# A gated mixer whose recurrence levels run between the half chunks of its input projection

## The reference, cut to what matters

```
h = rms_norm(x, mix_norm[l]) @ w_mix_in[l]                  # 256 x 1024 @ 1024 x 3336
(c_x, c_b, c_c, h_q, h_f, h_i, h_g, f_q, f_k, f_v, f_f) = split(h)
y = concat(short_conv(c_x, c_b, c_c),                       # 256 columns
           hgrn2(h_q, h_f, h_i, h_g),                       # 4 heads of 64, a gated recurrence
           fox(f_q, f_k, f_v, f_f))                         # 8 heads of 64, forgetting attention
x = x + y @ w_mix_out[l]

hgrn2:  S_t = diag(f_t) S_{t-1} + (1 - f_t)^T v_t,   o_t = q_t S_t
        out = rms_norm(o, gain) * silu(g)
fox:    q, k = rms_norm per head;   s[t, s'] = q_t . k_s' + c_t - c_s'   (c = cumsum log f)
        out = softmax(causal(s)) @ v
short_conv: c_b * causal_conv3(c_c * c_x)
```

## Time and profile before

| | us |
|---|---|
| median of 3 runs | 2005.02 |
| the profiled execution, its own time | 2008.44 |
| its span | 2007.1 |
| PE busy | 1850.7 (92%) |
| DVE busy | 1022.5 (51%) |
| ACT busy | 837.9 (42%) |
| POOL busy | 27.4 (1%) |

### The profile page before, as it was taken

One profiled execution on the slowest core, in us unless ns is written; L12 is line 12 of the kernel. 1 busy time (PEld: TensorE's weight loads), 2 busy tenths in 40 slices (PEclk: granted clock), 3 DMA queues, 4 the chain that ended last, 5 costly groups with the idle time before them and its releaser, 6 DMA issues.

```text
span 2007.1 us, 21477 instructions
## 1 busy us (share of the span) xinstructions
PE 1850.7 (92%) x8492; PEld 1453.1 (72%) x8492; DVE 1022.5 (51%) x1212; ACT 837.9 (42%) x1004; POOL 27.4 (1%) x51
## 2 busy tenths in 40 slices
PE   5998789988888999899999888999999998889999
PEld 3765667766556778688788667888888877668887
DVE  2726544324566544555455745554555457536543
ACT  3326434323344444354445434444444346325441
POOL 0000000000000000000000100000000000000000
PEclk8999799989898999999999759999999999569999
DMA  9652267745452765465554203655565554005651
GB/s 338 224 194 78 64 207 255 266 176 207 166 180 84 229 216 191 130 214 181 189 176 160 84 1 100 199 185 188 170 189 187 189 161 160 16 21 168 189 189 63
DMA packets 239597, 330.31 MB, mean 165 GB/s; under 512 B 11205, under 2 KB 192089, under 8 KB 239497
## 3 DMA queue, kind: packets, MB, share of 16 engines
q1 hardware_dynamic: 235872, 321.95, 48.6%
q10 hardware_dynamic: 2890, 5.39, 0.8%
q0 software_dynamic: 736, 1.60, 0.3%
HBM read 327.85 MB, written 1.05 MB: 164 GB/s over the span
## 4 chain that ended last, share of the span: by engine, by line
PE 82%; DVE 9%; ACT 4%; DMA 3%; issue 2%; SPq 0%; DVEq 0%; ACTq 0%
PE bank L398 16%; PE bank L400 16%; PE bank L399 16%; PE bank L675 7%; PE bank L676 7%; PE bank L678 7%; DVE lo L1666 2%; PE bank L422 2%; ACT hi L1106 2%; DMA raw<-in_ffn_w 1%; PE bank L739 1%; PE bank L927 1%; PE bank L1013 1%; PE bank L991 1%; PE bank L990 1%
## 5 line engine op out<-in xcount | busy, mean ns | idle before, releaser
L1666 DVE TENSOR_TENSOR lo<-raw,hi 128x2048 fp32r<-128x2048 f32 x258 | 590.2, 2291 | 612.2 <-ACT hi L1106 612.2
L1106 ACT ACTIVATE hi<-raw 128x2048 fp32r<-128x2048 f32 x258 | 492.3, 1912 | 477.1 <-PE bank L400 174.9
L398 PE MATMUL bank<-hi,XTh 128*128 128x512 f32 (+1 forms) x1424 | 566.7, 398 | 8.7 <-DVE XTl L1693 8.7
L399 PE MATMUL bank<-lo,XTh 128*128 128x512 f32 (+1 forms) x1424 | 554.8, 390 | 0.0
L400 PE MATMUL bank<-hi,XTl 128*128 128x512 f32 (+1 forms) x1424 | 554.8, 390 | 0.0
L398 PEld LDWEIGHTS bank<-hi,XTh 128*128 128x128 f32 x1424 | 270.4, 190 | 79.3 <-issue 14.8
L400 PEld LDWEIGHTS bank<-hi,XTl 128*128 128x128 f32 x1424 | 269.7, 189 | 56.8
L399 PEld LDWEIGHTS bank<-lo,XTh 128*128 128x128 f32 x1424 | 270.6, 190 | 52.3 <-issue 0.2
L675 PE MATMUL bank<-hi,HTh 128*128 128x512 f32 x528 | 211.0, 400 | 10.6 <-DVE HTl L1693 10.6
L676 PE MATMUL bank<-lo,HTh 128*128 128x512 f32 x528 | 208.6, 395 | 0.0
L678 PE MATMUL bank<-hi,HTl 128*128 128x512 f32 x528 | 164.8, 394 | 0.0
(11 more groups left out here) (331 smaller groups left out, 1520.4 us busy)
## 6 DMA issues: line engine op xcount, KB each, us to landing
raw<-in_ffn_w_in SPq DMA_DIRECT2D x176, 512.0 KB, 4.8
raw<-in_ffn_w SPq DMA_DIRECT2D x132, 512.0 KB, 6.0
raw<-in_ada_w SPq DMA_DIRECT2D x96, 512.0 KB, 6.1
raw<-in_ffn_w_out SPq DMA_DIRECT2D x88, 512.0 KB, 4.1
raw<-in_w_mix_in SPq DMA_DIRECT2D x52, 512.0 KB, 4.7
raw<-in_od_pw_w SPq DMA_DIRECT2D x24, 512.0 KB, 6.4
raw<-in_ev_w_in SPq DMA_DIRECT2D x20, 512.0 KB, 6.4
raw<-in_w_mix_out SPq DMA_DIRECT2D x16, 512.0 KB, 4.0
```

The costliest lines, as they stand in the source:

```text
L398: pe.matmul(dst, xh, wh, start=start, stop=False)
L399: pe.matmul(dst, xh, wl, start=False, stop=False)
L1106: act.activation(hi[r][:, :], raw[g % RING][:, :], ACT.Copy).then_inc(*up("hi", d))
L1666: dve.tensor_tensor(lo[r][:, :], raw[g % RING][:, :], hi[r][:, :].bitcast(F32), ALU.subtract).then_inc(*up("lo", d))
```

## The change

The columns of the projection are taken in another order (`MIX_COLS`): h_q and h_f first, then f_q and f_k, then c_x with c_b, c_c with h_i, and f_v; h_g is the last 256. The generators are gone: `mix` is written out on each engine, and on PE a fixed place after each half chunk holds what followed the projection before. POOL makes three of the `lo` operands (slabs d+9, d+11, d+13), and waits no longer for slab d+12 to be used. The scratch tiles `EX`, `TM`, `QKa`, `QKb` and `EXP` move out of the activation's operand `XTh` to places that are free during the projection, and `TMP` is replaced by `TN` in place.

```diff
+MIX_COLS = [(768, 1024), (1792, 2048), (2304, 2560), (0, 256), (512, 1280), (2816, 3072)]
+MIX_LAST = 1536
+
+POOL_LOW = (9, 11, 13)
...
-        EX, TM, QKa, QKb, EXP, TMP = (tile_at(f"hg_{n}", [P, 2, S], scr_at + 2048 * n) for n in range(6))
+        EX, TM = (tile_at(f"hg_e{n}", [P, 2, S], row_at + 2048 * n) for n in range(2))
+        QKa, QKb, EXP = (tile_at(f"hg_qk{n}", [P, 2, S], ht_at + 34816 + 2048 * n) for n in range(3))
...
-                jobs = background([fox_decay(l), hgrn_decay(l)])
...
+                for s in range(2, 12):
+                    c = s // 2
+                    if s % 2 == 0 and c >= 2:
+                        pe.wait_ge(*at("um_act", (l, c - 2)))
+                        pe.wait_ge(*at("um_dve", (l, c - 2)))
+                    if s == 10:
+                        pe.wait_ge(*at("c3_turned", (l, 1)))
+                    half_chunk(d + s, s % 2, x_groups(c))
+
+                    if s == 2:
+                        hgrn_turn(l)
+                    elif s == 4:
+                        fox_decay(l)
+                        pe.wait_ge(*at("hg_z", l))
+                        pe.wait_ge(*at("hg_k2t", l))
+                        hgrn_products(l, 0, K2, Q2, 4)
+                    elif s == 6:
+                        pe.wait_ge(*at("fox_c", l))
+                        hgrn_level(l, 1)
+                    elif s >= 7:
+                        hgrn_level(l, s - 5)
+                    if s == 8:
+                        pe.wait_ge(*at("um_act", (l, 3)))
+                        pe.wait_ge(*at("um_dve", (l, 3)))
+                        conv_turn(l, 1, 2)
+                    elif s == 10:
+                        pe.wait_ge(*at("um_act", (l, 4)))
+                        pe.wait_ge(*at("um_dve", (l, 4)))
+                        pe.wait_ge(*at("fox_normed", (l, 1)))
+                        fox_turn(l, 0, 0)
+                        fox_turn(l, 2, 1)
+                pe.wait_ge(*at("fox_q", (l, 0)))
+                pe.wait_ge(*at("fox_k", (l, 0)))
                 r = ready(d + 12)
...
-                for step in [h, f, h, c, f, h, c, f, h, c] + [h, f] * 16 + [f] * 20:
-                    next(step, None)
+                pe.wait_ge(*at("hg_sel", (l, 5, 1)))
+                fox_scores(l, 0)
+                fox_scores(l, 1)
...
+                hgrn_products(l, 7, K1, Q1, 2)
+                pe.wait_ge(*at("hg_sel", (l, 6, 1)))
+                fox_turn(l, 1, 4)
+                fox_turn(l, 3, 5)
...
+                conv_turn(l, 0, 0)
...
+                for u in range(N):
+                    if u + 2 < N:
+                        fox_scores(l, u + 2)
+                    if u >= 1:
+                        fox_values(l, u - 1)
+                    fox_turn_p(l, u)
+                    if u == 0:
...
+                        hgrn_products(l, 8, K1, Q1, 0, cross=True)
+                    elif u == 2:
+                        hgrn_values(l)
```

ACT's program has, at unit 6 of the loop, the gate and the root of hgrn's norm together:

```diff
+                    elif u == 6:
+                        act.wait_ge(*at("um_dve", (l, 6)))
+                        act.activation(GS[:, :, :], UM[:, :, o_hg:o_hg + HALF], ACT.Silu).then_inc(*up("hg_silu", l))
+                        act.wait_ge(*at("hg_var", l))
+                        act.activation(ST[:, 8:16], ST[:, 8:16], ACT.Sqrt).then_inc(*up("hg_std", l))
```

DVE's program, from the scan to the last chunk, and POOL's:

```diff
+                select(l, 0, 7, 4)
+                split(d + 8)
+                rows_of(2)
+                hgrn_level(l, 1)
+                hgrn_level(l, 2)
+                split(d + 10)
+                select(l, 1, 1, 6)
+                hgrn_level(l, 3)
...
+                rows_of(3)
+                select(l, 2, 2, 4)
+                hgrn_level(l, 4)
+                split(d + 12)
...
-                pool.wait_ge(*at("used", first[f"up{4 + 3 * l}"] + 12))
+                d = first[f"up{4 + 3 * l}"]
...
-                    if lv == 1:
+                    if lv == 2:
...
+                        split(d + 9)
+                    elif lv == 3:
+                        split(d + 11)
+                    elif lv == 5:
+                        split(d + 13)
```

More of the change, by code:

```diff
@@ L207, in weight_slabs @@
                 w = A["w_mix_in_2"][l, :, :]
-                chunks(f"up{p}", 6, w, 0, w, HALF, CH)
-                wide_slab(w, 3072)
+                first[f"up{p}"] = len(dense)
+                for a, b in MIX_COLS:
+                    for half in range(2):
+                        up_slab(w, a, w, b, half)
+                wide_slab(w, MIX_LAST)
                 p += 1
@@ new lines, in hgrn_products @@
+            def hgrn_products(l, i, lhs, rhs, b, cross=False):
+                for h in range(HG_H):
+                    for t in range(1 if cross else T):
+                        part = slice((h % 2) * HD, (h % 2 + 1) * HD)
+                        s_at, t_at = (0, P) if cross else (t * P, t * P)
+                        o = (2 * t + h // 2) * P
+                        last = pe.matmul(bank[b + h % 2][:, o:o + P], lhs[part, h // 2, s_at:s_at + P],
+                                         rhs[part, h // 2, t_at:t_at + P], start=True, stop=True)
+                last.then_inc(*up("hg_prod", (l, i)))
@@ L1066, in mix @@
[L1066 to L1067 removed]
+                first_chunk(p)
+                pe.wait_ge(*at("small2", (l, 2)))
+                for t in range(T):
+                    for k in range(KD):
+                        last = pe.matmul(bank[7][:, t * FOX_H:(t + 1) * FOX_H], FULL[:, k, tok[t]], WF[:, k, :],
+                                         start=(k == 0), stop=(k == KD - 1))
+                last.then_inc(*up("fox_z", l))
@@ new lines, in mix @@
+                N = len(fox_units)
+                for u in range(N):
+                    if u + 1 < N:
+                        fox_softmax(l, u + 1)
+                    if u == 0:
+                        split(d + 16)
+                    if u >= 1:
+                        fox_values(l, u - 1)
+                    if u == 2:
+                        conv_taps(l)
+                    elif u == 5:
+                        hgrn_heads(l, 0)
+                    elif u == 7:
+                        hgrn_heads(l, 1)
+                    elif u == 8:
+                        hgrn_heads(l, 2)
```

795 lines of the change are left out of this document (335 added, 460 removed).

## The result

The changed kernel takes 1973.5 us (median of four runs, 1970.5 to 1977.8), the kernel before 2006.2 in the same comparison: ratio 0.9833, 95% interval 0.982 to 0.9846, or 32.7 us less. Forecast were 23.0 us less, with a range of 1968 to 1997. The direction and the main mechanism were right and the time lies inside that range, but the gain was 1.4 times the sum, and the prediction's own narrower range, 1975 to 1990, was missed by 1.5 us.

A forecast was written before the change was run, and what follows sets the result against it. PE bounds the kernel, at the lower clock in the tails, plus about 15 us of waits there. Per mixer -23.2 + 9.1 + 2.6 = -11.5 us, -23.0 in all: 2005.0 to 1982 us; range 1975 to 1990, 8 in 10 1968 to 1997.

The forecast's parts named there:

- The clock in the projection: From the gate's products to slab d+12's end: clock 0.95 or more, levels 0 to 6 at 1.26 us each.
- the rival that it falls: Projection: small products between half chunks bring the clock down, making the kernel slower, 2014 us; chance 0.06.
- New waits, 2.6 us: Projection: PE waits for DVE's row copies before c_b's transposes, 0.9 us, and before fox's transposes, 1.7 us, each mixer.
- the first of the two places: Projection, c_b's transposes after half chunk 8: PE waits 0.9 us for chunk 3's row copy behind the norm's sum.
- Work put into the projection, 9.1 us: Projection: seven products add 8.4 us and twelve transposes 1.6, while a wait of 0.9 for h_q's copy goes.
- GpSimd's splits and the lock: Projection: each POOL split takes 4.1 us and can hold DVE that long; rival, held worse, 1993 us, chance 0.17.
- The tail's opening, 5.1 us: Tail before the loop: two units' scores 2.0 us, product 7 1.2, twelve transposes 1.6, fox's second query 0.3.
- Units 0 to 6, 21.2 us: Tail's loop: first seven units priced at 3.03 us each, the lower clock's price.
- the rival "the clock stays up": Tail: five units run at the upper clock, saving up to 1.2 us each, 6 a mixer; 1970 us, chance 0.15.
- The wait at unit 6, 2.5 us: Tail's loop: PE waits 2.5 us because ACT does gate and root together with three table loads.
- product 8's wait for DVE's last operands: Tail, unit 0: PE waits 1.3 us, since those operands stand behind fox's query, a selection and four small ones.
- The bound of the tail's second half: Tail, fox's units alone: bound by PE at the lower clock, 3.03 us a unit, not by the softmax.

The follow-up runs named there:

- e2: Changed kernel with recurrence levels 3 to 6 moved from the projection back into the tail's fox units 0 to 3: 1978.1 us, ratio 0.9849.
- e1: Changed kernel with GpSimd's three low-half splits per mixer given back to VectorE: 1972.6 us, ratio 0.9823.
- e7: Changed kernel with the keys' decay product left out of fox's scores, so part of the computation is missing: 1951.3 us, ratio 0.9722.
- e3: Changed kernel with the end of fox's norm and its sixteen transposes put after the projection again, ahead of the first scores: 1981.3 us, ratio 0.9868.
- e13: Changed kernel with one decay product a head, placed in the odd unit ahead, and the last slab's dense products in four parts: 1958.3 us, ratio 0.9756.
- e11: Changed kernel with one decay product a head, both units scored behind it, and the last slab in four parts: 1966.5 us, ratio 0.9798.
- e10: Changed kernel with the last slab's dense products in four parts, ahead of and behind the first scores and in units 0 and 1: 1964.9 us, ratio 0.9793.
- e5: Changed kernel with the last slab's dense products in four parts, one in each of units 0 to 3: 1970.1 us, ratio 0.9820.
- e0: The changed kernel run again unaltered, beside other experiments: 1971.0 us, ratio 0.9814.
- e12: Changed kernel with one decay product a head, the next head's decay placed in the odd unit ahead: 1963.4 us, ratio 0.9783.
- e6: Changed kernel with ScalarE's Silu moved into the projection and its Sqrt into unit 14, out of unit 6: 1974.6 us, ratio 0.9833.

## Why the prediction came out as it did

Term by term, for the first mixer:

- **The clock in the projection**: right, and the rival that it falls was wrong. 1.00 in the first mixer and 0.98 in the second, with all seven levels at 1.26 us between half chunks. The Trainium skill's section on depth-cycling ("TensorE: Matmul & The Clock Gate"), which spoke for this rival, found nothing to act on: it speaks of small pauses of TensorE, there were none, and the eight pieces cost no clock. The 1.6 us behind the gate's products were missing in one mixer of the changed kernel; I had left them in the sum.
- **New waits, 2.6 us**: the step that failed. TensorE waited nowhere in the projection. Chunk 4's row copy on DVE was done at 1105.3 (L2227, 1104.54 + 0.74), fox's transposes came at 1108.4, 3.1 us later, where I had DVE 1.7 us behind. So my layout put DVE late by 5 us. It counted half chunks of 5.45 us, where a half chunk with its level takes 6.7, and that is the likely error, though no run tests the layout itself. e2 fits that: with the later slots empty a wait of 1.3 us stands at the first of the two places.
- **Work put into the projection, 9.1 us**: it was some 10. With 69.1 - 1.6 (what was missing behind the gate's products) + 9.1 it would be 76.6, and it was 77.5. The 0.9 us fit the changes between the kinds of product, for which I had nothing: 1106.90 to 1107.22 is 0.32 us where dense products follow at 0.227.
- **GpSimd's splits and the lock**: the mechanism was right, the size small. 4.6, 4.6 and 5.3 us instead of 4.1, and DVE's instructions held for 4.5 and 2.4 us. The rule that I cited from the Trainium skill ("SBUF — State Buffer", "Who interferes with whom") speaks, as I put it, of VectorE instructions with two SBUF inputs. The multiply of 4.5 us is one. The 2.36 us instruction has one input and was held as well, and so has the one of 0.89 us in the earlier trace rows, so that row doesn't bear out the rule in my words. The same section says that a `tensor_scalar` can contend too, in modes that use two ports; no row here shows the mode. But DVE had the room, and e1 settles that all of it costs nothing that can be measured.
- **The tail's opening, 5.1 us**: right, 5.12 (1122.12 to 1127.24).
- **Units 0 to 6, 21.2 us**: mis-sized, 17.6. I priced every unit at the lower clock, but it stayed up until 1131.9, for 9.7 us, and unit 0 and most of unit 1 are in it. What I had read in the earlier trace rows, a clock "still up" at 1129.8, was no evidence for this: the kernel before had lost it at 1117.6, in the pause of 6.2 us, and got it back at 1124.4 on small products alone (PE busy, PEclk, DMA share, GB/s):

```profile
1117.00:1118.00 1.00, 0.00 (x0) 0.80 1.04 363
...
1124.00:1125.00 1.00, 1.00 (x9) 0.79 0.36 80
```

  This is part of the rival "the clock stays up", of which the rest did not come: from unit 7 on a unit still takes 3.02 us. That rival's time, 1970, is nearer to the measured one than mine, by luck: it wanted five units at the upper clock and not quite two had it; the rest came from waits and from the gate's products.
- **The wait at unit 6, 2.5 us**: 1.13; product 8 took 0.6 us instead of 1.1 (upper clock again); product 8's wait for DVE's last operands was 0.48 instead of 1.3, and another of 0.96 at the head of unit 1, for DVE to read unit 1's scores out of their bank, was not in my sum, so the two together hit its size by luck; `HA` times h_i took 5.15, as forecast.
- **The bound of the tail's second half**: right in the main. e7 took 14.4 us of TensorE's work out and 10 came off.

Together: the projection 3.3 us and the tail 5.4 us below their sums, 8.7 a mixer, of which 2.6 + 1.6 - 0.9 and 3.6 + 1.4 + 0.5 - 0.1 are named above. The profiles then say -39 for the mixers, and the medians -33 to -37.

What the parts are worth, from the changed kernel: levels 3 to 6 in the projection 7 us of the 33 to 37, the norm's early place 7 to 10 (e3's profile has some 3 us of dips), GpSimd's share 0. The rest (the levels 0 to 2, h_g's copy no longer behind the norm) wasn't tried alone; that the 6.2 us wait of the earlier trace rows went is seen in the trace.

## What to carry to other kernels

Work that must be done anyway is cheapest where the clock is at its upper level and the engines that make its operands have room: the same eight products cost 1.26 us between dense products and 2.24 in the tail. Before pricing a stretch behind dense work, read the granted clock microsecond by microsecond: two products timed at two places don't say what lies between them, and a pause that the change removes can have cost clock too. When a loop is bound by TensorE, look for instructions that repeat their fixed cost (two products on the same row became one), and give each step of the loop a piece of work between a transpose and the product that needs its copy (e13 against e11).

## What the hardware showed that was not expected

- Dense products placed between the small ones held the clock up: in e10 it didn't fall before 1139.3, 5.3 us past the last of them. In e5, where it had fallen before, it rose at 1130.1, 3.8 us after the first dense part began, and held until 1147.1; whether they brought it back is open.
- The clock fell for 3.4 us and rose again with TensorE busy and nothing dense under way (e0, 1689.6 to 1693.0). The same dip stands in both mixers of e12 and in the second of e6, and, behind a pause of 2.5 us, in both of e3. Such dips move a mixer by 1.5 us from one execution to the next.
- A VectorE instruction of 32 columns took 2.36 us, and one of 256 columns 4.52 us (0.41 by itself), beside a GpSimd instruction of 2048 columns, and both ended within 0.3 us of its end.
